# Memory, parameters and meta rows loaded with features on the partitions, and an opening by single tiles, in a two-block float32 kernel on one core

## The reference, cut to what matters

```python
# first block, x (256, 2048), mem (256, 2048), float32
h = rmsnorm(x, norm_g)
... = split_cols(h @ w_in, IN_SIZES)
m_k, m_v = split(rmsnorm(mem, mem_norm_g) @ w_mem_kv, 2)   # w_mem_kv (2048, 1024)
kc = rmsnorm(m_k.reshape(256, 4, 128), k_norm_c);  vc = m_v
...                                                        # three attentions, gates
x = x + merged @ w_o
# second block
h = concat([meta, x])                                      # 16 meta rows ahead of x
u = rms_norm(h, g_pre_mix)
...                                                        # pools, convolution, mlp
```

## Time and profile before

| | us |
|---|---|
| median of three runs | 2054.8 (2054.5 to 2054.82) |
| the profiled execution, its own time | 2054.71 |
| its span, first to last instruction | 2052.9 |
| PE busy | 2040.2 (99%) |
| DVE busy | 1356.1 (66%) |
| ACT busy | 947.2 (46%) |

### The profile page before, as it was taken

The page is one execution under the profiler, slowest core; times in us unless marked ns, Lnnn a source line. Parts: engine busy times, 40 slices in busy tenths (PEclk is TensorE's granted clock), DMA queues, the critical chain, the costliest instruction groups (busy, mean ns, idle before and its releaser), DMA issues.

```text
span 2052.9 us, 29398 instructions
## 1 busy us (share of the span) xinstructions
PE 2040.2 (99%) x10629; PEld 1738.2 (85%) x10629; DVE 1356.1 (66%) x1811; ACT 947.2 (46%) x1223; POOL 81.3 (4%) x90
## 2 busy tenths in 40 slices
PE   9999999999999999999999999999999999999998
PEld 7888898888788888999888888888888888888886
DVE  6666766566756655578999856577557546646655
ACT  6545444565544444433444644553333333333343
POOL 0000102001002000002000000000000000000000
PEclk9999999999999999999999999999999999999999
DMA  8688555555566555555666565655565665565653
GB/s 301 195 184 196 178 155 171 193 166 180 178 206 233 187 185 187 171 175 160 194 190 198 182 234 186 205 161 183 199 190 180 199 192 181 194 194 184 194 192 106
DMA packets 265823, 387.02 MB, mean 189 GB/s; under 512 B 12411, under 2 KB 147417, under 8 KB 265180
## 3 DMA queue, kind: packets, MB, share of 16 engines
q1 hardware_dynamic: 262828, 374.83, 57.6%
q0 software_dynamic: 2576, 10.41, 2.0%
q10 hardware_dynamic: 304, 0.27, 0.0%
HBM read 382.79 MB, written 2.54 MB: 188 GB/s over the span
## 4 chain that ended last, share of the span: by engine, by line
PE 97%; DVE 1%; SPq 1%; DMA 1%; ACT 1%; issue 0%; DVEq 0%; ACTq 0%
PE acc L605 19%; PE acc L607 19%; PE acc L606 19%; PE acc L628 17%; PE acc L626 10%; PE acc L620 2%; PE acc L618 2%; PE acc L619 2%; PE acc L624 1%; DMA stage_rows<-in_w_mem_kv 1%; PE aux L1563 1%; PE aux L1479 1%; PE acc L548 0%; PE acc L547 0%; PE acc L546 0%
## 5 line engine op out<-in xcount | busy, mean ns | idle before, releaser
L489 DVE TENSOR_TENSOR low_rows<-stage_rows,high_rows 128x1024 fp32r<-128x1024 f32 x440 | 542.8, 1237 | 412.0 <-ACT high_rows L478 406.6
L478 ACT ACTIVATE high_rows<-stage_rows 128x1024 fp32r<-128x1024 f32 x440 | 464.6, 1059 | 583.3 <-PE acc L607 531.9
L489 DVE TENSOR_TENSOR w_low<-stage,w_high 128x1024 fp32r<-128x1024 f32 (+1 forms) x264 | 320.0, 1219 | 236.0 <-ACT w_high L478 232.3
L478 ACT ACTIVATE w_high<-stage 128x1024 fp32r<-128x1024 f32 (+1 forms) x264 | 276.2, 1047 | 420.0 <-PE acc L628 302.8
L628 PE MATMUL acc<-u,w_high 128*128 128x512 f32 x900 | 248.0, 395 | 0.0
L605 PE MATMUL acc<-high_rows,f_pair 128*128 128x512 f32 x496 | 193.2, 390 | 0.0
L606 PE MATMUL acc<-low_rows,f_pair 128*128 128x512 f32 x496 | 193.2, 389 | 0.0
L607 PE MATMUL acc<-high_rows,f_pair 128*128 128x512 f32 x496 | 193.2, 389 | 0.0
L628 PE MATMUL acc<-hT,w_high 128*128 128x512 f32 x645 | 177.5, 394 | 0.0
L628 PEld LDWEIGHTS acc<-u,w_high 128*128 128x128 f32 x900 | 153.1, 189 | 18.8
L626 PEld LDWEIGHTS acc<-u,w_low 128*128 128x128 f32 x960 | 146.9, 189 | 20.4
(11 more groups left out here) (414 smaller groups left out, 3356.5 us busy)
## 6 DMA issues: line engine op xcount, KB each, us to landing
stage_rows<-in_w_in SPq DMA_DIRECT2D x160, 512.0 KB, 3.6
stage<-in_w_in SPq DMA_DIRECT2D x136, 512.0 KB, 3.5
stage_rows<-in_w_down SPq DMA_DIRECT2D x128, 512.0 KB, 4.3
stage<-in_w_up SPq DMA_DIRECT2D x120, 512.0 KB, 3.8
stage_rows<-in_w_o SPq DMA_DIRECT2D x64, 512.0 KB, 3.6
stage_rows<-in_w_mem_kv SPq DMA_DIRECT2D x16, 512.0 KB, 9.0
stage_rows<-in_w_pool_out SPq DMA_DIRECT2D x16, 512.0 KB, 4.1
stage_rows<-in_w_conv_out SPq DMA_DIRECT2D x16, 512.0 KB, 4.5
```

Source lines behind the costliest of these rows:

```text
L478: act.activation(high[:, pr, 0:kt, 0:p.cols], src[:, slot, 0:kt, 0:p.cols], ACT.Copy).then_inc(high_done, 1)
L489: dve.tensor_tensor(low[:, pr, 0:kt, 0:p.cols], src[:, slot, 0:kt, 0:p.cols], high[:, pr, 0:kt, 0:p.cols].bitcast(F32), ALU.subtract).then ...
```

## The change

The host hands over four further arrays: `params`, all parameters as columns on 128 partitions, `rel_bias_t`, `mem_t` (128 partitions x 16 feature groups x 256 tokens) and `meta_t`. `mem_t` is loaded straight into place, so PE's turns of `mem`, of the parameters and of the meta rows go, with the copies behind them. ACT and DVE now make the pair of `mem` from SBUF (`high_mem`, `low_mem`).

The slabs of `mem_kv` are taken in turns for the first half: columns of `m_k` and `m_v` of the same rows follow each other (`in_turns=8`), so that a piece of `mem` serves two slabs. The first slab and the first piece of memory come by single tiles of 128 rows.

The squares of memory still want tokens on the partitions. So the rows of `mem` are loaded a second time, 2 x 1 MB into `mem_in`, which lies where `mem_t` lies. SP waits for the last memory unit to be made (`pair_ready` 8) ahead of that, behind the issue of slab 11. The squares of `x` move from n = 5 and 6 to 7 and 8, those of memory from 8 and 9 to 11 and 12. In `w_up_c` the last two units move by one slab.

```diff
         self.pieces = [(p, pn, sum(p.slabs[:q]), kt, q == len(p.slabs) - 1) for pn, p in enumerate(parts) for q, kt in enumerate(p.slabs)]
+        if in_turns:
+            self.pieces.sort(key=lambda piece: (piece[2], piece[1]) if piece[2] < in_turns else (in_turns + piece[1], piece[2]))
...
-                  "w_up_c": (13, [(3, 10, 13), (10, 14, 17), (14, 20, 23)])}
+                  "w_up_c": (13, [(3, 10, 13), (10, 15, 18), (15, 21, 24)])}
...
-        MEM_AFTER = {1: [(4, 256, 512)], 2: [(1, 512, 1024)], 3: [(2, 1024, 1536)], 5: [(3, 1536, 2048)]}
-        X_AFTER = {5: (0,), 6: (1,), 7: (2, 3)}
...
+        MEM_AFTER = {1: [(4, 2, 4)], 3: [(1, 4, 8)], 4: [(2, 8, 12)], 5: [(3, 12, 16)]}
+        MEM_TURN_AT = {0: 1, 2: 2, 4: 3, 5: 4, 6: 5, 7: 6, 8: 7}
+        X_AFTER = {6: (0,), 7: (1,), 8: (2,), 9: (3,)}
...
-            ("mem_kv", Job(2, [by_rows(A["w_mem_kv"], 0, [2] * 8, mem_pair, ("pair_ready", 0))], 2)),
+            ("mem_kv", Job(1, [by_rows(A["w_mem_kv"], c * ROW, [2] * 8, mem_pair, ("pair_ready", 0)) for c in range(2)], 1, in_turns=8)),
...
             def other_params():
...
+                sp.dma_start(params[:, N0:PARAMS], A["params"][:, N0:PARAMS]).then_inc(s("params_in"), 16)
+                sp.dma_start(relT[:], A["rel_bias_t"]).then_inc(s("params_in"), 16)
                 sp.dma_start(sinks, A["sinks_b"].partition_broadcast(P)).then_inc(s("sinks_in"), 16)
...
+                        if n == 0:
+                            for k in range(2):
+                                sp.dma_start(mem_t[:, k, :], A["mem_t"][:, k, :]).then_inc(s("mem_in5" if k else "mem_in0"), 16)
+                                sp.dma_start(stage_rows[:, 0, k, :], A["w_mem_kv"][k * P:(k + 1) * P, 0:ROW]).then_inc(s("first_in") if k == 0 else landed[0], 16)
+                            sp.sem_inc(issued, 1)
+                        else:
...
+                            sp.dma_start(mem_t[:, lo:hi, :], A["mem_t"][:, lo:hi, :]).then_inc(s(f"mem_in{c}"), 16)
...
+                        if n in (11, 12):
+                            if n == 11:
+                                sp.wait_ge(s("pair_ready"), 8)
+                            t = n - 11
+                            sp.dma_start(mem_in[:, t, :], A["mem"][t * P:(t + 1) * P, :]).then_inc(s(f"mem_rows_in{t}"), 16)
...
+            def high_mem(k):
+
+                act.activation(mem_pair[:, k, 0, :], mem_t[:, k, :], ACT.Copy, scale=column("mem_norm_g", k)).then_inc(s("pair_high"), 1)
+
+            def high_mem_unit(q):
+
+                if q == 1:
+                    act.wait_ge(s("mem_in4"), 16)
+                elif q % 2 == 0:
+                    act.wait_ge(s(f"mem_in{q // 2}"), 16)
+                for k in (2 * q, 2 * q + 1):
+                    high_mem(k)
...
+            act.wait_ge(s("params0_in"), 16)
+            act.wait_ge(s("mem_in0"), 16)
+            high_mem(0)
+            act.wait_ge(s("first_in"), 16)
+            act.activation(high_rows[:, 0, 0, :], stage_rows[:, 0, 0, :], ACT.Copy).then_inc(s("pair_high"), 1)
+            act.wait_ge(s("mem_in5"), 16)
+            high_mem(1)
+            act.wait_ge(landed[0], 16)
+            act.activation(high_rows[:, 0, 1, :], stage_rows[:, 0, 1, :], ACT.Copy).then_inc(high_done, 1)
...
-                if n in (5, 6):
-                    if n == 5:
+                if n in (7, 8):
+                    if n == 7:
                         act.wait_ge(s("x_in"), 64)
                     else:
                         act.wait_ge(s("input_squared"), 1)
-                    row_squares(x_in, "x", n - 5, "input_squared")
-                if n == 7:
+                    row_squares(x_in, "x", n - 7, "input_squared")
+                if n == 8:
...
-                    row_squares(mem_in, "mem", n - 8, "input_squared")
                 if n == 10:
-                    act.wait_ge(s("params_copied"), 5)
+                    act.wait_ge(s("params_in"), 32)
...
+                if n in (11, 12):
+                    act.wait_ge(s(f"mem_rows_in{n - 11}"), 16)
+                    act.wait_ge(s("input_squared"), n - 9)
+                    row_squares(mem_in, "mem", n - 11, "input_squared")
...
+            pe.wait_ge(s("mem_in0"), 16)
+            keep_running(4, 2)
+            pe.wait_ge(s("first_in"), 16)
+            keep_running(4, 2)
+
+            def first_products(k):
+                if k == 0:
+                    pe.wait_ge(s("first_unit"), 2)
+                    return
+                pe.wait_ge(split_done, STAGES + 1)
+                pe.wait_ge(s("pair_ready"), 1)
...
-                if n == META_AT:
-                    pe.wait_ge(s("meta_in"), 16)
-                    pe.wait_ge(s("merged_ready"), 8)
-                    for k in range(KT):
-                        mm = pe.transpose(aux[:, 0, k * META:(k + 1) * META], meta_in[:, k * P:(k + 1) * P], ident[0:META, 0:META])
-                    mm.then_inc(s("meta_turned"), 1)
...
-                dve.tensor_copy(relT[:], aux[0:NB, 3, 3 * P:3 * P + BUCKETS]).then_inc(s("params_copied"), 1)
-                dve.wait_ge(s("params_copied"), 5)
...
+            def low_mem(k, done):
+
+                return dve.scalar_tensor_tensor(out=mem_pair[:, k, 1, :], in0=mem_t[:, k, :], scalar=column("mem_norm_g", k),
+                                                in1=mem_pair[:, k, 0, :].bitcast(F32), op0=ALU.mult, op1=ALU.subtract).then_inc(done, 1)
+
+            def low_mem_unit(q):
+
+                dve.wait_ge(s("pair_high"), 2 * q + 3)
+                low_mem(2 * q, s("mem_low"))
+                dve.wait_ge(s("mem_low"), q)
+                low_mem(2 * q + 1, s("pair_ready"))
...
-                if n == 12:
+                if n == 13:
                     dve.wait_ge(s("input_squared"), 4)
                     chain_var(1, ("mem", 0, own("mem", 2), 1.0 / D, EPS))
```

More of the change, by code:

```diff
@@ L578, in first_by_tile, with multiply @@
                     between(t, idx)
-        def multiply(pe, job, i, u, beside=None, between=None):
+        def multiply(pe, job, i, u, beside=None, between=None, first_slab=None):
             for idx, (p, part, k0, kt, last) in enumerate(job.pieces):
@@ L1324, in _, with products @@
         def _(pe):
-            def products(name, beside=None, between=None):
+            def products(name, beside=None, between=None, first=None):
                 job = jobs[name]
@@ L1328, in products @@
                     for step in range(job.steps):
-                        multiply(pe, job, step // job.unroll, step % job.unroll, beside, between)
+                        multiply(pe, job, step // job.unroll, step % job.unroll, beside, between, None if step else first)
                     return
@@ L1740, in low_unit, with first_low_rows @@
                 dve.sem_inc(s("pair_ready"), 1)
-            for q in range(4):
+            def low_mem(k, done):
[6 more added lines that the diff above has]
+                low_mem(2 * q + 1, s("pair_ready"))
+            def first_low_rows(k, done):
+                dve.tensor_tensor(low_rows[:, 0, k, :], stage_rows[:, 0, k, :], high_rows[:, 0, k, :].bitcast(F32), ALU.subtract).then_inc(done, 1)
+            dve.wait_ge(s("pair_high"), 1)
+            low_mem(0, s("first_unit"))
+            dve.wait_ge(s("pair_high"), 2)
+            first_low_rows(0, s("first_unit"))
+            dve.wait_ge(s("pair_high"), 3)
+            low_mem(1, s("pair_ready"))
+            dve.wait_ge(high_done, 1)
+            first_low_rows(1, split_done)
+            for q in range(1, 4):
                 subtract_low(dve, jobs["mem_kv"], 0, 0, q)
-                if q < 2:
-                    low_unit(mem_pair, "mem_norm_g", q, 0)
+                if q == 1:
+                    low_mem_unit(1)
             def splitting(name, body, links=0, beside=None, at_once=False):
@@ L1761, in lead_mem @@
             def lead_mem(n):
[L1762 to L1763 removed]
+                if n and n in MEM_TURN_AT:
+                    low_mem_unit(MEM_TURN_AT[n])
             def beside_mem(n):
[L1766 removed]
+                if n == 8:
                     dve.wait_ge(s("input_squared"), 2)
@@ L2451, in _, with by_features, laid_out @@
                     link(dve.scalar_tensor_tensor(out=eps_3, in0=eps_3, scalar=EPS, in1=eps_3, op0=ALU.mult, op1=ALU.mult))
-_NAMES = ["x", "mem", "norm_g", "w_in", "kv_norm_g", "w_kv_up", "idx_k_ln_g", "idx_k_ln_b", "q_norm_a", "k_norm_a",
-          "q_norm_b", "k_norm_b", "sinks_b", "mem_norm_g", "w_mem_kv", "q_norm_c", "k_norm_c", "w_up_a", "w_up_b",
-          "w_up_c", "gate_bias", "w_o", "rel_bias", "meta_2", "g_pre_mix_2", "w_in_2", "w_pool_grp_2", "pool_scale_2",
-          "w_pool_out_2", "w_dw_2", "b_dw_2", "conv_ln_g_2", "conv_ln_b_2", "w_conv_out_2", "w_o_2", "g_post_mix_2",
-          "g_pre_mlp_2", "w_up_2", "w_down_2", "g_post_mlp_2"]
+_NAMES = ["x", "mem", "w_in", "w_kv_up", "sinks_b", "w_mem_kv", "w_up_a", "w_up_b", "w_up_c", "gate_bias", "w_o", "meta_2", "w_in_2",
```

(14 more changed lines are left out.)

114 lines of the change are left out of this document (29 added, 85 removed).

## The result

The changed kernel takes **2063.5 us** (median of 6 runs, 2063.2 to 2064.2) against 2054.8 for the kernel before beside it (6 runs). The ratio is 1.0043, 95% interval 1.0032 to 1.0054: 0.4% slower, 8.7 us. The forecast was 2061.0, with a range from 2057.0 to 2065.5. The profiled execution took 2063.47 us with a span of 2061.3, 8.4 us longer than the span of before.

The account below looks back on a forecast made before the run. PE was taken to bound the kernel, busy 2040.2 of 2052.9 us, with transfers scarce early. Terms 6.4 + 0.5 + 2.0 - 1.4 - 1.2 = +6.3 on 2054.71 gave 2061.0 us, range 2057.0 to 2065.5.

Parts of the forecast that it names:

- The signs: Profile marks expected: first product near 5.9, PE idle about 12 us before x's turn near 50, clock at half there.
- Part 1: PE in the opening: first product at 5.9, 2.8 earlier; slab 10 done at 38.0, 5.6 earlier, deciding nothing.
- Part 2: Chain to x's first turn: slab 10 landing at 31.0, slab 12 at 43.6, turn at 50.0, 6.4 us later.
- Part 3: From x's turn to ikw: ACT's memory squares and the wait for the first eviction add 0.5 us, bounds 0 and 1.5.
- Part 4: PE's clock after idling about 12 us before x's turn: half rate for four us, +2.0 us, bounds 0 and 2.5.
- Part 5: Later places: PE's probabilities wait in w_up_c goes, -1.4 us; the meta turn of w_o goes, -1.2 us.
- The landing of slab 12 is later still: Rival in the opening: transfers issued behind slab 12 take their share, adding up to 2.7 us: 2063.7; chance 0.1.
- The clock holds: Rival at x's turn: the clock stays up, or ACT covers the slow matmuls: 2059.0; chance 0.17.
- the wait is short: Rival: slab 10 at 29.5, slab 12 overtakes memory rows, x turned at 46, clock holds: 2055.0; chance 0.14.
- the change doesn't do what it says: Rival in the opening: first products no earlier, at 8.7, the time still 2061; no chance given.
- Faster: Rival: x's chain no longer holds PE at slab 11, ikw starts 5.6 earlier, 2.6 saved later: 2046.5; chance 0.06.
- The sum: Whole kernel: delays and savings from opening to end total +6.3 us, giving 2061.0.

Follow-up runs that it names:

- run 1: Changed kernel with memory's rows landing in the unused upper half of hT, so the queue no longer waits for memory's last pair: 2056.0 us.
- run 5: Changed kernel with memory's units 2 to 7 worked out one or two slabs sooner, the queue's wait kept: 2057.3 us.
- run 3: Changed kernel with both squares of x, root and scaling one slab sooner, the queue's wait kept: 2064.0 us.
- run 2: Changed kernel with 80 transposes of the identity on PE ahead of its wait for x's scaled rows: 2062.1 us.
- run 8: Changed kernel with memory's rows in hT, issued later without the queue's wait, and x's squares two slabs sooner; memory's units left late: 2055.3 us.
- run 9: run 7 with memory's column groups one after the other again in place of in turns: 2056.7 us.
- run 10: run 8 with 8 transposes of the identity on PE after slab 0 and 8 after slab 9: 2053.3 us.
- run 7: Changed kernel with memory's units sooner, its rows in hT, issued later without the queue's wait, and x's squares, root and scaling two slabs sooner: 2049.5 us.
- run 6: Kernel before with only the new places of w_up_c, nothing else of the change: 2053.2 us.

## Why the prediction was right, point by point

- **Direction and mechanism: right.** One idle time of PE ahead of the first turn of `x`, its cause the chain SP's wait, slab 12, second square. The signs came: 10.65 us idle in place of about 12, the turn at 51.90 in place of 50, slab 12 on ACT at 45.57 in place of 43.6, the clock at half ahead of the turn. Runs 1 and 5 each took hold of the chain at another place and gave back 7.4 and 6.2 us. Run 3 showed that the squares' place gives nothing while SP's wait stands.
- **Part 1, PE done with slab 10 at 38.0: wrong by 3.2, and without effect,** as the prediction says. The last product starts at 40.86 and ends at 41.25. The first product came at 5.53, sooner than the 5.9. But slab 0's first six products go some 0.43 us apart, and slab 1 starts only at 11.06, since its weights are rounded from 8.60 and split behind that. The kernel before had slab 1 at 11.95. Of the 3.2 us that the first product gains, 0.9 are left one slab later. This is what I missed: single tiles bring the first product forward, not the second slab.
- **Part 2, slab 10 at 31.0: the term that was mis-sized.** ACT got it at 32.50, above both of my ends (30.3 and 31.9). I had counted bytes from the start at the same pace as before. The windows of the first 10 us, of before and of after, show that pace to be lower:

```profile
0.00:10.00 10.00, 7.06 (x37) 5.83 (x38) 3.54 (x6) 5.50 (x9) 1.71 (x11) 1.00 0.75 262
```

```profile
0.00:10.00 10.00, 7.42 (x25) 5.47 (x25) 2.57 (x5) 4.71 (x7) 1.72 (x11) 1.00 0.75 219
```

  The 43 GB/s less are 430 KB in 10 us, by my estimate 1.1 us at 385 GB/s. Why the queue is slower there wasn't tried. From slab 10 on the links hold: the last pair is done at 39.05, 6.55 behind slab 10 (6.3 forecast), slab 12 is rounded 6.5 behind the pair (6.3 forecast), the turn comes 6.33 behind slab 12 (6.4 forecast). The mark came 8.28 later, not 6.4, and 1.5 of the 1.9 between them are in that first link. The prediction also calls the transfers the scarce thing from 20 to 25 us. The same row has PE busy for 5.00 of 5.00 us: both were full there.
- **Part 3, +0.5: small by 0.4.** With the full clock there, runs 2, 8, 9 and 10 have 18.05 to 18.13 us from the turn to `ikw`, against 17.22: +0.9, of which 0.7 are PE's wait for the eviction. Run 7 has 18.51. It stood within the bounds.
- **Part 4, +2.0 for the clock: right.** 20.03 less 18.13 is 1.9, by run 2. Which idle time brings it was seen too generously: I took the 12 us as the reason, and 4.33 us were enough in run 1.
- **Part 5, -1.4 and -1.2: right.** The places gave 1.6 in both kernels. The meta turn is worth 1.3: from the first to the last product of `w_o` it is 90.44 us in the kernel after and 91.78 in that of before and in run 6. The two together are 2.9, of which 2.69 came out.
- **The rivals.** "The landing of slab 12 is later still" at 2063.7 comes nearest in its number, but not by its mechanism: slab 12 took 6.5 us from the end of SP's wait, as in the forecast without this rival. It was the end of the wait that was late. "The clock holds", "the wait is short" and "the change doesn't do what it says" fell (0.50 ahead of the turn, the turn at 51.90, first product at 5.53). "Faster" was right on its condition, a turn of `x` before 41.7: in run 7 it is 39.66, and the time 2049.5.
- **The sum:** +8.28 + 2.81 - 2.69 = 8.4, where 6.4 + 2.5 - 2.6 = 6.3 was forecast. The range was written wider than its own terms give: 2061.0 less 2.0, 0.7 and 0.5 is 2057.8, not 2057.0, and 2061.0 with 2.7, 1.0 and 0.5 is 2065.2, not 2065.5. The measured 2063.5 lies within either.

## What to carry to other kernels

A wait on the engine that issues the transfers costs what is queued behind it, not what it protects: here one buffer shared by memory's columns and its rows held the queue for 14 us, the weights of four slabs behind it, while the transfer engines stood still for 6 us. Before putting a load behind such a wait, look for an address that is free at the time. And where a stage is sped up at its head, follow the second and third item of each queue, not the first: the gain is only what the last of them keeps.

## What the runs showed of the hardware

The granted clock fell to half behind waits much shorter than the 12 us I had argued with. At slab 1 it fell behind waits of 1.98, 2.17 and 3.49 us (runs 1, 8, 9) and not behind waits of 0.92, 1.25, 1.32 and 1.77 us (run 5, run 10, the changed kernel, run 2). It did not fall behind 1.74 us at slab 4 (the changed kernel) nor behind 2.12 us at slab 10 (run 8). Behind 4.33 and 6.45 us at the turn of `x` (runs 1 and 5) and 4.98 us at slab 12 (run 3) it was down. These are single executions and give no rule. Where PE's wait of 10.7 us was filled with 8.9 us of transposes of the identity, it did not fall (run 2).

The times of the kernels whose traces show such a fall at slab 1 spread over 3.5 to 5 us (runs 1, 8, 9), those of the kernel before over 0.7. But runs 2 and 10, with the full clock at slab 1 in their traces, spread over 4.4 and 3.0 us. So the clock is shown as a cost of some 2 us, by runs 2 and 10, and not as the reason for the scatter.

In the changed kernel the first six products go some 0.43 us apart, half the pace, though the windows print a granted clock of 1.00. So the printed clock does not tell the pace of the first microseconds. The distance of the starts does.
